# Second-layer attention of a six-layer kernel: score blocks by residue class of the query, laid between projection tiles

## Chip, cores and metric

One core of a Trainium2 chip runs one program. The metric is the device time of one execution in microseconds (us); lower is better.

## The reference, cut to what matters

Six layers, 512 tokens, width 1024, all in fp32. The change is in the second layer alone (`mixer_b`). It has 8 heads of 128 channels, and each head attends three times, with queries, keys and values of its own for each of three patterns (group g):

```python
B_PATTERNS = ((128, 1), (512, 4), (2048, 16))     # window, dilation
for g, (window, dilation) in enumerate(B_PATTERNS):
    q = apply_partial_rotary(rms_norm(qkv[:, :, 0, g], q_gain[g]), cos, sin)
    k = apply_partial_rotary(rms_norm(qkv[:, :, 1, g], k_gain[g]), cos, sin)
    o, lse = dilated_window_attention(q, k, qkv[:, :, 2, g], window // dilation, dilation)
wgt = jax.nn.softmax(jnp.stack(lses), axis=0)
o = jnp.einsum('gbsh,gbshd->bshd', wgt, jnp.stack(outs))
y = o.reshape(bsz, S, B_WIDTH).astype(h.dtype) * jax.nn.silu(z)
return y @ w_out
```

Query t of group g attends keys t - j * dilation, j = 0 to window // dilation = 128, if they exist. So group 0 ("near") sees the 129 latest tokens, group 1 every fourth token back to 512, group 2 every sixteenth. Weighting the three results by the softmax of their log-denominators equals one softmax over the union of the three groups' scores, and so the kernel does it. For groups 1 and 2 a query needs only keys of its own residue class modulo 4.

## The kernel before, in words

**Engines and signals.** Every engine has its own program, in an order written out by hand; each operation raises its engine's semaphore (`did`), and others wait for the count of an event by name (`of`). Projection weights come in 1 MB panels (1024 x 256), each a DMA on SP's queue into one of three slots of `Wr` (L326, when the panel three before is used). ACT casts a panel to `Wh` (L1225), POOL subtracts the remainder `Wl` (L344, four instructions), PE multiplies. `ahead(name)` in the ACT and POOL programs is that split, of the panel two after the one named. Products of activations and weights are three fp32r matmuls (high x high, high x low, low x high: `mm3`, L536 to L538). `tile_f` (24 matmuls of 512 columns) makes 128 features x 512 tokens in one PSUM bank; `tile_t` (48 of 256 columns; tokens are the stationary operand) makes 2 x 128 tokens x 256 features. PSUM has 8 banks: `ps` 0 to 3 and `psx` (4 to 7); `into(b)` makes PE wait until bank b is emptied.

**The second layer** runs over four pairs of heads, i = 0 to 3, each in three stages:

1. Queries and keys: 12 tiles (t = 4g + 2 * is-key + head), banks in rotation over four. ACT squares and copies each (`sq`, `tmp`, L1441, L1446), PE sums the squares over partitions with a matmul of ones (L743), ACT takes the root (L1414), DVE the reciprocal (L2008), the product with gain (L2013), the swapped half for the rotary (L2020, L2022), POOL the rest of the rotation (`rope`, L398, L401). Results are `QB` and `KB`, [channel, group, head, token].
2. Values: 6 tiles (3 groups x 2 halves of the tokens), banks in rotation over four, copied by DVE to `VB` (L2057).
3. Attention and gates. Units are (head, block j of 128 queries), j = 3 down to 0. A unit has min(2, j+1) near blocks and j+1 of each other group, 10, 8, 6 and 3 blocks of 128 x 128 (27 a head). `scores` (L760) writes them to banks 4 to 6 with one matmul a run of blocks; DVE adds the mask from `maskB` and takes the maximum (L2031), ACT the exponential with row sums (L1420), DVE the division (L2040, L2042). `flip` (L773) transposes up to four blocks into bank 7, 2 or 3, DVE and ACT in turn copy them to `tmp` (L2072, L1470), `values` (L787) multiplies with `VB` into bank 0 or 1. The next unit's scores are issued one unit ahead. The first gate tile (`z`) follows unit 0's scores, the second stands before unit 4's transposes; ACT applies silu (L1426). At the end of a head DVE multiplies with the gate (L2046), ACT casts to `Yh` (L1485), DVE subtracts to `Yl` (L1880).

Stage 1 of the next pair starts only when stage 3 is done. After the fourth pair comes the output projection `out` (8 tiles over 4 panels).

The fourth layer's attention, which the prediction also reads, contracts over 64 channels; its scores (L977) are matmuls on channels 0 to 63 and 64 to 127 of the same tiles, one of 512 and one of 256 columns in each pair. In the fifth sublayer's convolution PE transposes every second token of `wH` (L1123), an 8-byte step in its stationary operand; L1049 has such a stationary operand too, and DVE's L2395 steps by 8 bytes.

Of the kernel before, what the change touches and what calls it, by code (L numbers as in the profile page):

```python
# [104 lines left out]
B_BLOCKS = [min(2, j + 1) + 2 * (j + 1) for j in range(TT)]  # L105
B_MASK_AT = [sum(B_BLOCKS[:j]) * P for j in range(TT)]


def blocks_of(j):
    return [(0, t) for t in range(max(0, j - 1), j + 1)] + [(g, t) for g in (1, 2) for t in range(j + 1)]  # L110


B_UNITS = [(hh, j) for hh in range(2) for j in reversed(range(TT))]
B_GROUPS = [(u, q0) for u, (hh, j) in enumerate(B_UNITS) for q0 in range(0, B_BLOCKS[j], 4)]
# [69 lines left out]
def setting(nc, ctx, I):  # L184
# [38 lines left out]
    with ExitStack() as over:  # L223
# [5 lines left out]
        E.QB, E.KB, E.VB, E.maskB, E.PB, E.ropeB, E.stB = phase(  # L229
            ("QB", [P, 3, 2, S], F32), ("KB", [P, 3, 2, S], F32), ("VB", [P, 3, TT, 256], F32),  # L230
            ("maskB", [P, 27 * P], BF16), ("PB", [P, 2304], F32), ("ropeB", [32, 2, S], F32),
            ("stB", [P, TT, 4], F32))
# [23 lines left out]
    E.wsr = E.vst[:].rearrange("p a n -> p (a n)").rearrange("p (g n) -> p g n", g=8)  # L256
    E.QD, E.KD, E.VD = (E.QD0, E.QD1), (E.KD0, E.KD1), (E.VD0, E.VD1)
# [76 lines left out]
def pool_program(E, pool):  # L334
# [58 lines left out]
    def rope(i, t):  # L393
        g, qk, f = t // 4, t // 2 % 2, t % 2
        q = (E.KB if qk else E.QB)[0:32, g, f, :]
        spare = E.acc[0:32, :] if t % 2 else tmp[0:32, 3, :]
        pool.wait_ge(*V.of("B", "swap", i, t))
        pool.tensor_tensor(q, q, E.ropeB[:, 0, :], ALU.mult).then_inc(*G.did("B", "cos", i, t))  # L398
# [118 lines left out]
def pe_program(E, pe):  # L517
# [36 lines left out]
    def tile_t(p, pair, hi, lo, b, event, emptied_by, ready=None):  # L554

        into(b)
        for j, t in enumerate(pair):
            for k in range(KD):
                if ready:
                    pe.wait_ge(*ready(k))  # L560
                m = mm3(bank[b][:, j * 256:(j + 1) * 256], hi[:, k, t * P:(t + 1) * P], lo[:, k, t * P:(t + 1) * P],
                        part(E.Wh, p, k, 0, 256, KD), part(E.Wl, p, k, 0, 256, KD), k == 0, k == KD - 1)
        m.then_inc(*T.did(*event))
        emptied[b] = emptied_by
# [169 lines left out]
    def mixer_b():  # L734
        QB, KB, VB, PB = E.QB, E.KB, E.VB, E.PB
        turn = (7, 2, 3)
        norm_sums("B", "A0")

        def ssq(i, t):
            r = t % 2  # L740
            into(6 + r)
            pe.wait_ge(*A.of("B", "sq", i, t))
            pe.matmul(psx[:, 2 + r, :], ones[:], sq[:, r, :], start=True, stop=True).then_inc(*X.did("B", "ssq", i, t))  # L743
            emptied[6 + r] = A.of("B", "sqrt", i, t)

        def scores(i, u):
            hh, j = B_UNITS[u]
            for b in (4, 5, 6):
                into(b)
            if u == 0:  # L750
                pe.wait_ge(*G.of("B", "rope", i, 11))
                pe.wait_ge(*V.of("B", "v", i, 2, 1))
            runs = []
            for pos, (g, t) in enumerate(blocks_of(j)):
                if runs and runs[-1][1] == g and pos % 4:
                    runs[-1][3] += 1
                else:
                    runs.append([pos, g, t, 1])
            for pos, g, t, c in runs:
                m = pe.matmul(psf[:, pos * P:(pos + c) * P], QB[:, g, hh, j * P:(j + 1) * P], KB[:, g, hh, t * P:(t + c) * P],  # L760
                              start=True, stop=True)
            m.then_inc(*X.did("B", "s", i, u))
            for b in (4, 5, 6):
                emptied[b] = V.of("B", "sc", i, u)

        def flip(i, n):
            u, q0 = B_GROUPS[n]
            j = B_UNITS[u][1]
            po, w, b = (0 if j % 2 == 0 else 1024) + q0 * P, min(4, B_BLOCKS[j] - q0), turn[n % 3]
            into(b)  # L770
            pe.wait_ge(*V.of("B", "pn", i, u))
            for r in range(w):
                m = pe.transpose(bank[b][:, r * P:(r + 1) * P], PB[:, po + r * P:po + (r + 1) * P], ident[:])  # L773
            m.then_inc(*X.did("B", "flip", i, n))
            X.also("B", "flipped", i, u)
            emptied[b] = (A if n % 2 else V).of("B", "fe", i, n)

        def values(i, n):
            u, q0 = B_GROUPS[n]
            hh, j = B_UNITS[u]  # L780
            bl = blocks_of(j)
            if q0 == 0 and u % TT == 0:
                into(hh)
            pe.wait_ge(*(A if n % 2 else V).of("B", "fe", i, n))
            for pos in range(q0, min(q0 + 4, len(bl))):
                g, t = bl[pos]
                m = pe.matmul(bank[hh][:, j * P:(j + 1) * P], VB[:, g, t, hh * P:(hh + 1) * P],  # L787
                              tmp[:, n % 4, (pos % 4) * P:(pos % 4 + 1) * P], start=(pos == 0), stop=(pos == len(bl) - 1))
            m.then_inc(*X.did("B", "pv", i, n))
            if q0 + 4 >= len(bl) and u % TT == TT - 1:  # L790
                emptied[hh] = V.of("B", "yz", i, hh)

        for i in range(4):
            t, nb = 0, 0
            for g in range(3):
                for qk in range(2):
                    p = begin("B", "qk", i, g, qk)
                    if i + t == 0:
                        first_f("B", p, (0, 1), [("B", "qk", 0, f) for f in range(2)], [A.of("B", "cp", 0, f) for f in range(2)])
                    for f in range(2):  # L800
                        if i or t >= 2:
                            tile_f(p, f, Ah, Al, (nb + f) % 4, ("B", "qk", i, t), A.of("B", "cp", i, t))
                        if t:
                            ssq(i, t - 1)
                        t += 1
                    used(p)
                    nb += 2
            for g in range(3):
                p = begin("B", "v", i, g)
                for u in range(2):  # L810
                    tile_t(p, (2 * u, 2 * u + 1), Ah, Al, (nb + u) % 4, ("B", "v", i, g, u), V.of("B", "v", i, g, u))
                    if g + u == 0:
                        ssq(i, 11)
                used(p)
                nb += 2
            scores(i, 0)
            p = begin("B", "z", i)
            tile_f(p, 0, Ah, Al, nb % 4, ("B", "z", i, 0), A.of("B", "z", i, 0))
            for n in range(len(B_GROUPS) + 2):
                if n < len(B_GROUPS):  # L820
                    u, q0 = B_GROUPS[n]
                    if q0 == 0 and u + 1 < len(B_UNITS):
                        scores(i, u + 1)
                    if q0 == 0 and u == TT:
                        tile_f(p, 1, Ah, Al, (nb + 1) % 4, ("B", "z", i, 1), A.of("B", "z", i, 1))
                        used(p)
                    flip(i, n)
                if n >= 2:
                    values(i, n - 2)
            X.also("B", "end", i)  # L830
        T.also("h_end", "B")
        out("B", 0)
# [383 lines left out]
def act_program(E, act):  # L1216
# [180 lines left out]
    def mixer_b():  # L1397
# [3 lines left out]
        HM = 27 * P // 2  # L1401
        scale = 1.0 / float(np.sqrt(P))
        gate("A0")
        act.dma_start(PB[:, 0:HM], I["k_maskB"][:, 0:HM]).then_inc(*LDB.did(0))
        act.dma_start(qf[:, 0:HM], I["k_maskB"][:, HM:2 * HM]).then_inc(*LDB.did(1))
        act.dma_start(ropeB[:], I["k_ropeB"]).then_inc(*LDB.did(2))
        norm("B", E.Ah, "A0", summed=None)

        def sqrt(i, t):
# [4 lines left out]
            act.activation(rs[:, r, :], psx[:, 2 + r, :], ACT.Sqrt, bias=eps[:, 0:1], scale=1.0 / P).then_inc(*A.did("B", "sqrt", i, t))  # L1414

        def exp(i, u):
            hh, j = B_UNITS[u]
            po, w = 0 if j % 2 == 0 else 1024, B_BLOCKS[j] * P
            act.wait_ge(*V.of("B", "nm", i, u))
            act.activation(PB[:, po:po + w], PB[:, po:po + w], ACT.Exp, bias=stB[:, j, 1:2], scale=scale,  # L1420
                           accum_out=stB[:, j, 2:3]).then_inc(*A.did("B", "exp", i, u))

        def gates(i, f):
            act.wait_ge(*T.of("B", "z", i, f))
            act.wait_ge(*X.of("B", "ssq", i, 10 + f))
            act.activation(sq[:, f, :], ps[2 + f][:], ACT.Silu).then_inc(*A.did("B", "z", i, f))  # L1426

        for i in range(4):
            t = 0
            for g in range(3):  # L1430
                for qk in range(2):
                    for f in range(2):
                        if t:
                            sqrt(i, t - 1)
                        b = t % 4
                        act.wait_ge(*T.of("B", "qk", i, t))
                        if t >= 2:
                            act.wait_ge(*X.of("B", "ssq", i, t - 2))
                        elif i:
# [1090 lines left out]
```

## Time and profile before

| what | us |
|---|---|
| median of 3 runs (lowest, highest) | 3273.06 (3268.32, 3273.66) |
| span of the profiled execution, core 0 | 3272.5 |
| PE busy, L536 to L538, L760, L773, L787 among it | 3198.1 |
| DVE, ACT, POOL busy | 1645.0, 1102.3, 1564.8 |
| second layer, sums of squares to the output projection | 441 to 1061 |

The profile gives for the profiled execution only its span, 3272.5 us from first to last instruction, and no separate device time. A row's `L760` is the line in the kernel; `psx<-KB,QB` is output and inputs by name, the moving operand first; `x240` counts records. PE is matmuls, PEld weight loads, which overlap them. An fp32 matmul appears as two records, an fp32r one or a transpose as one. A record of a matmul is longer than the distance to the next, since they are pipelined; the pace is read from starts.

### The profile page before, as it was taken

What the parts mean: (1) busy time and instruction counts of PE and PEld (TensorE: products, weight loads), DVE (VectorE), ACT (ScalarE), POOL (GpSimd) and SP (SyncE); (2) the same over time, 40 slices, a digit from 0 to 9 for tenths busy, and PEclk for the clock granted to TensorE, in tenths of its full rate; (3) what the DMA queues carried; (4) which work ended last, traced back from release to release, by engine and by line L of the source; (5) the groups of instructions that cost most, each with busy time, mean ns of one, the idle gap of its engine ahead of it and who ended that gap; (6) DMA issues with size and microseconds to landing.
All of it is one profiled execution on the core that took longest, in us unless ns stands there. A gap on an engine that the chain in (4) does not pass through costs nothing.

```text
span 3272.5 us, 39766 instructions
## 1 busy us (share of the span) xinstructions
PE 3198.1 (98%) x16422; PEld 2643.4 (81%) x16422; DVE 1645.0 (50%) x2141; ACT 1102.3 (34%) x1449; POOL 1564.8 (48%) x1138
## 2 busy tenths in 40 slices
PE   8999999999999999999999999999999999999998
PEld 7988878787878888899887877766888867778887
DVE  6753575757474443544546666665212266542223
ACT  3221243434343332333222434444222343242222
POOL 4444475556464455454433511126545466344544
PEclk9999999999999999999999999999999999999999
DMA  5554422211221232345444211112333332223332
GB/s 165 163 165 142 142 101 65 78 65 65 65 77 53 90 103 91 103 142 179 153 147 145 70 39 39 41 37 77 104 97 97 100 124 82 80 65 94 99 96 72
DMA packets 279317, 320.07 MB, mean 98 GB/s; under 512 B 6866, under 2 KB 245089, under 8 KB 278946
## 3 DMA queue, kind: packets, MB, share of 16 engines
q1 hardware_dynamic: 240960, 247.48, 23.6%
q10 hardware_dynamic: 38178, 70.06, 6.4%
q8 instruction: 130, 2.13, 0.3%
q14 instruction: 49, 0.40, 0.0%
HBM read 311.22 MB, written 6.29 MB: 97 GB/s over the span
## 4 chain that ended last, share of the span: by engine, by line
PE 90%; DVE 4%; ACT 2%; POOL 1%; issue 1%; DMA 1%; ACTq 0%; SPq 0%; DVEq 0%
PE ps L536 25%; PE ps L538 24%; PE ps L537 24%; PE psx L977 2%; PE psx L743 1%; PE ps L1009 1%; POOL Wl L344 1%; PE ps L787 1%; PE psx L721 1%; PE psx L536 1%; PE psx L537 1%; PE psx L538 1%; PE psx L636 1%; PE psx L760 1%; PE psx L688 1%
## 5 line engine op out<-in xcount | busy, mean ns | idle before, releaser
L344 POOL TENSOR_TENSOR Wl<-Wr,Wh 128x512 fp32r<-128x512 f32 x928 | 1281.5, 1413 | 1506.5 <-ACT Wh L1225 1502.4
L536 PE MATMUL ps<-Ah,Wh 128*128 128x512 f32 x1920 | 771.5, 402 | 0.7 <-POOL Wl L344 0.7
L538 PE MATMUL ps<-Ah,Wl 128*128 128x512 f32 x1920 | 748.4, 390 | 0.0
L537 PE MATMUL ps<-Al,Wh 128*128 128x512 f32 x1920 | 747.9, 390 | 0.0
L1225 ACT ACTIVATE Wh<-Wr 128x2048 fp32r<-128x2048 f32 x232 | 443.0, 1910 | 368.6 <-DMA Wr<-in_w_mlp_in_dram 109.8
L536 PEld LDWEIGHTS ps<-Ah,Wh 128*128 128x128 f32 x1920 | 360.7, 188 | 85.0 <-issue 11.1
L537 PEld LDWEIGHTS ps<-Al,Wh 128*128 128x128 f32 x1920 | 360.7, 188 | 83.3 <-issue 10.3
L536 PE MATMUL ps<-Yh,Wh 128*128 128x512 f32 x1088 | 425.1, 391 | 0.1
L537 PE MATMUL ps<-Yl,Wh 128*128 128x512 f32 x1088 | 423.8, 390 | 0.0
L538 PE MATMUL ps<-Yh,Wl 128*128 128x512 f32 x1088 | 423.7, 389 | 0.0
L538 PEld LDWEIGHTS ps<-Ah,Wl 128*128 128x128 f32 x1920 | 360.4, 188 | 76.6
L536 PE MATMUL ps<-Wh,Ah 128*128 128x256 f32 x896 | 257.6, 288 | 3.3 <-DVE vA L1936 3.3
L538 PE MATMUL ps<-Wh,Al 128*128 128x256 f32 x896 | 253.5, 283 | 0.0
L537 PE MATMUL ps<-Wl,Ah 128*128 128x256 f32 x896 | 253.4, 283 | 0.0
L536 PEld LDWEIGHTS ps<-Yh,Wh 128*128 128x128 f32 x1088 | 204.7, 188 | 42.8 <-issue 0.4
L538 PEld LDWEIGHTS ps<-Yh,Wl 128*128 128x128 f32 x1088 | 204.5, 188 | 42.8
L537 PEld LDWEIGHTS ps<-Yl,Wh 128*128 128x128 f32 x1088 | 204.6, 188 | 41.9
L1924 DVE SCALAR_TENSOR_TENSOR macc<-modw,sc,macc 128x512 f32<-128x512 f32 x168 | 166.3, 990 | 115.3 <-DMA modw<-in_w_mod_dram 108.8
L2008 DVE RECIPROCAL rs<-rs 128x512 f32<-128x512 f32 x48 | 160.6, 3346 | 44.3 <-ACT rs L1414 44.2
L536 PEld LDWEIGHTS ps<-Wh,Ah 128*128 128x128 f32 x896 | 171.8, 192 | 5.6 <-issue 5.6
L537 PEld LDWEIGHTS ps<-Wl,Ah 128*128 128x128 f32 x896 | 171.9, 192 | 1.9 <-issue 1.9
L538 PEld LDWEIGHTS ps<-Wh,Al 128*128 128x128 f32 x896 | 171.9, 192 | 0.0
(405 smaller groups left out, 4157.7 us busy)
## 6 DMA issues: line engine op xcount, KB each, us to landing
Wr<-in_a_w_in_dram SPq DMA_DIRECT2D x48, 1024.0 KB, 6.7
modw<-in_w_mod_dram ACTq DMA_DIRECT2D x96, 512.0 KB, 5.5
Wr<-in_b_w_in_dram SPq DMA_DIRECT2D x40, 1024.0 KB, 5.0
Wr<-in_w_mlp_in_dram SPq DMA_DIRECT2D x32, 1024.0 KB, 5.5
Wr<-in_w_mlp_out_dram SPq DMA_DIRECT2D x32, 1024.0 KB, 5.1
Wr<-in_a_w_out_dram SPq DMA_DIRECT2D x16, 1024.0 KB, 5.2
Wr<-in_c_w_in_dram SPq DMA_DIRECT2D x16, 1024.0 KB, 5.6
Wr<-in_attn_w_qkv_dram SPq DMA_DIRECT2D x12, 1024.0 KB, 5.2
```

The lines of the kernel that those rows point to most:

```text
L344: last = pool.tensor_tensor(E.Wl[:, s, part], E.Wr[:, s, part], E.Wh[:, s, part].bitcast(F32), ALU.subtract)
L536: pe.matmul(o, ah, bh, start=first, stop=False)
L537: pe.matmul(o, ah, bl, start=False, stop=False)
L538: return pe.matmul(o, al, bh, start=False, stop=last)
L636: pe.matmul(psx[:, 2, 0:cols], ones[:], sq[:, k % 2, 0:cols], start=(k == 0), stop=(k == KD - 1)).then_inc(*X.did(*event))
L688: m = pe.matmul(psx[:, 1, c:c + 1], t[:, r * P:(r + 1) * P], ones[:, 0:1], start=True, stop=True)
L721: m = pe.matmul(psx[:, 2 * f, t * P:(t + 1) * P], E.vst[:, f, t * P:(t + 1) * P], E.wsT[:, q, :], start=True, stop=True)
L743: pe.matmul(psx[:, 2 + r, :], ones[:], sq[:, r, :], start=True, stop=True).then_inc(*X.did("B", "ssq", i, t))
L977: m = pe.matmul(psf[:, c:c + k1 - k0], q[64 * r:64 * r + 64, h, j * P:(j + 1) * P], k[64 * r:64 * r + 64, h, k0:k1], start=True, stop=True)
L1225: act.activation(E.Wh[:, s, :], E.Wr[:, s, :], ACT.Copy).then_inc(*HI.did(p))
L1924: dve.scalar_tensor_tensor(t, w, E.sc2[:, k, who:who + 1], t, ALU.mult, ALU.add).then_inc(*V.did("mac", L, nb, who, k))
L2008: dve.reciprocal(rs[:, r, :], rs[:, r, :]).then_inc(*V.did())
```

## The change

Units become (head, residue class r of the query modulo 4), 8 a pair of heads. A unit's 128 queries are the tokens 4n + r. Groups 1 and 2 need one block each, the keys of class r; the near group needs, for each quarter q of the unit's queries (32 of them, tokens 128q to 128q + 127), the token blocks q - 1 and q (0 and 1 for q = 0, masked). That is four blocks a unit, 16 a head, and one PSUM bank. The near scores are four matmuls of 32 stationary columns each, one for each quarter, into partitions 32q to 32q + 31.

To this end `QB` (all groups) and `KB` (groups 1 and 2) are stored class by class, by a stepped read in DVE's product; near keys stay in token order, and the rotary tables are ordered by class. The values of groups 1 and 2 are computed by `tile_t` with the tokens of a class (every fourth) as stationary operand. The mask is 4 x 512 columns a partition in place of 3456.

The order changes: units stand between the last four value tiles and the two gate tiles; the last two units' transposes and values of a pair, and its second head's output, stand between the first three query tiles of the next pair (`tail`), for the fourth pair inside the output projection, whose first three tiles are cut by k into 0 to 5, 6 and 7. Query and key tiles rotate over banks 0 to 2, value tiles over 0 and 1, gates take 0 and 1, the heads' outputs 2 and 3, scores and sums of squares 4 and 5, transposes 6 and 7. ACT alone empties the transposes; it copies the gate tiles out and applies silu to both at the end of the stage. DVE multiplies output and gate with stepped access. The POOL program has the same steps; only the near keys' rotation is stepped.

The diff, cut to its core:

```diff
+def by_class(ap):
+    return ap.rearrange("a (r n) -> a r n", r=4)
+def by_token(ap):
+    return ap.rearrange("a (n r) -> a r n", r=4)
+def near(ap, q):
+    return ap.rearrange("a (r q n) -> a q r n", r=4, q=4)[:, q]
# POOL, rope
-        pool.tensor_tensor(q, q, E.ropeB[:, 0, :], ALU.mult)
+        turn = by_token if qk and g == 0 else by_class
+        pool.tensor_tensor(turn(q), turn(q), by_class(E.ropeB[:, 0, :]), ALU.mult)
# PE
+        def qk(i, t):
...
+                tile_f(p, f, Ah, Al, t % 3, ("B", "qk", i, t), A.of("B", "cp", i, t))
...
+            if t:
+                ssq(i, t - 1)
+        def value(i, n):
+            g, u = n // 2, n % 2
...
+            if g:
+                tile_t(p, (2 * u, 2 * u + 1), Ah, Al, u, event, V.of(*event), lambda a, r: by_token(a)[:, r])
+            else:
+                tile_t(p, (2 * u, 2 * u + 1), Ah, Al, u, event, V.of(*event))
+        def scores(i, u):
+            hh, r = u // 4, u % 4
+            b, c0 = 4 + u % 2, u % 4 * P
+            into(b)
+            if r == 0:
+                pe.wait_ge(*G.of("B", "rope", i, 10 + hh))
+            for q in range(4):
+                t = max(q - 1, 0)
+                pe.matmul(bank[b][32 * q:32 * q + 32, 0:256], QB[:, 0, hh, c0 + 32 * q:c0 + 32 * q + 32], KB[:, 0, hh, t * P:(t + 2) * P], start=True, stop=True)
+            for g in (1, 2):
+                m = pe.matmul(bank[b][:, (g + 1) * P:(g + 2) * P], QB[:, g, hh, c0:c0 + P], KB[:, g, hh, c0:c0 + P], start=True, stop=True)
+        def far(i, u):
...
+            for g in (1, 2):
+                pe.matmul(bank[2 + hh][:, r * P:(r + 1) * P], VB[:, g, r, hh * P:(hh + 1) * P], E.PT[hh][:, r, (g + 1) * P:(g + 2) * P],
+                          start=(r == 0 and g == 1), stop=False)
+        def close(i, hh):
+            for q in range(4):
+                for c in range(2 if q else 1):
+                    t = max(q - 1, 0) + c
+                    m = pe.matmul(near(bank[2 + hh], q), VB[:, 0, t, hh * P:(hh + 1) * P], E.PT[hh][:, :, c * P + 32 * q:c * P + 32 * q + 32],
+                                  start=False, stop=(q == 3 and c == 1))
+        def tail(i, n):
+            if n < 2:
+                flip(i, 6 + n)
+                far(i, 5 + n)
+            if n == 2:
+                far(i, 7)
+                close(i, 1)
         for i in range(4):
+            for t in range(12):
+                qk(i, t)
+                if i:
+                    tail(i - 1, t)
+            value(i, 0)
+            ssq(i, 11)
+            value(i, 1)
+            for n in range(B_UNITS):
+                if n < 4:
+                    value(i, n + 2)
+                elif n % 2 == 0:
+                    gate(i, n // 2 - 2)
+                scores(i, n)
+                if 1 <= n < 7:
+                    flip(i, n - 1)
+                if n == 4:
+                    far(i, 0)
+                    far(i, 1)
+                elif n == 5:
+                    far(i, 2)
+                    far(i, 3)
+                    close(i, 0)
+                elif n == 6:
+                    far(i, 4)
+        for c in range(3):
+            part_out(c, 0, 6)
+            tail(3, c)
+        for c in range(3):
+            part_out(c, 6, 7)
+        for c in range(3):
+            part_out(c, 7, 8)
# DVE
+            near_keys = qk and g == 0
+            put = by_token if near_keys else by_class
-            dve.scalar_tensor_tensor(dst, tmp[:, t % 3, :], pk(E, "b_k_gain" if qk else "b_q_gain", g), rs[:, r, :],
+            dve.scalar_tensor_tensor(put(dst), by_token(tmp[:, t % 3, :]), pk(E, "b_k_gain" if qk else "b_q_gain", g), by_token(rs[:, r, :]),
         for i in range(4):
             for t in range(11):
                 rest(i, t)
+                if i and t == 1:
+                    y(i - 1, 1)
+            rest(i, 11)
+            for n in range(2):
+                value(i, n)
+            for n in range(B_UNITS):
+                if n < 4:
+                    value(i, n + 2)
+                scores(i, n)
+                weights(i, n)
+            y(i, 0)
```

## Rows read from the trace of the kernel before

**Rows 1.** The page: busy time by engine, and the granted clock in 40 slices.

```profile
PE 3198.1 (98%) x16422; PEld 2643.4 (81%) x16422; DVE 1645.0 (50%) x2141; ACT 1102.3 (34%) x1449; POOL 1564.8 (48%) x1138
PEclk9999999999999999999999999999999999999999
```

**Rows 2.** Stretches: length, busy time (records) of PE, PEld, DVE, ACT, POOL, clock, DMA.

```profile
441.00:517.20 76.20, 76.20 (x356) 60.61 (x357) 69.00 (x57) 31.96 (x42) 65.96 (x46) 1.00 0.26 84
...
541.79:587.79 46.00, 42.12 (x271) 36.94 (x271) 21.87 (x50) 21.50 (x32) 6.88 (x6) 1.00 0.14 46
...
1014.60:1060.80 46.20, 42.06 (x271) 36.93 (x271) 21.97 (x51) 21.50 (x32) 6.58 (x5) 1.00 0.15 46
```

**Rows 3.** PE timeline around the first attention stage: start, duration, engine, line.

```profile
540.63 0.28 PE L538 MATMUL ps<-Wh,Al 128*128 128x256 f32 x1
...
543.83 0.58 PE L536 MATMUL ps<-Ah,Wh 128*128 128x512 f32 x1
...
549.49 1.89 PE L760 MATMUL psx<-KB,QB 128*128 128x256 f32 x8
...
587.74 0.48 PE L536 MATMUL ps<-Ah,Wh 128*128 128x512 f32 x1
```

**Rows 4.** Chain of waits: start, duration, what (x: records).

```profile
556.77 0.86 DVE PB L2031
557.86 1.04 ACT PB L1420 x2
559.12 0.63 DVE PB L2042
...
562.52 2.17 PE psx L760 x10
...
575.75 0.44 PE psx L773 x4
...
583.44 0.89 PE ps L787 x8
...
598.88 0.86 PE psx L743 x2
```

**Rows 5.** PE timeline at the end of the first value tile.

```profile
510.87 0.28 PE L537 MATMUL ps<-Wl,Ah 128*128 128x256 f32 x1
510.99 0.28 PE L538 MATMUL ps<-Wh,Al 128*128 128x256 f32 x1
511.11 1.02 PE L743 MATMUL psx<-sq,ones 128*128 128x512 f32 x2
```

**Rows 6.** DVE timeline: end of the query and key stage, and one product later.

```profile
512.89 3.35 DVE L2008 RECIPROCAL rs<-rs 128x512 f32<-128x512 f32 x1 [0.40 <-ACT rs L1414]
...
519.75 1.27 DVE L2057 COPY VB<-ps 128x512 f32<-128x512 f32 x2
...
610.24 0.75 DVE L2013 SCALAR_TENSOR_TENSOR QB<-tmp,PK,rs 128x512 f32<-128x512 f32 x1
```

**Rows 7.** PE and PEld timelines, fourth layer's first scores (split by 64 rows).

```profile
1874.25 2.33 PE L977 MATMUL psx<-KD,QD 64*128 64x512 f32 x8
1876.50 0.50 PE L536 MATMUL ps<-Ah,Wh 128*128 128x512 f32 x1
...
1875.44 0.30 PEld L977 LDWEIGHTS psx<-KD,QD 64*128 64x128 f32 x4 [0.90 <-PE psx L977]
```

**Rows 8.** Single lines: duration in ns least/median/most, first and last start.

```profile
L1123 PEld LDWEIGHTS psx<-ident,wH x32: 195/209/209, 2712.8 to 2779.4; 128*128 128x128 f32 x32
...
L773 PEld LDWEIGHTS psx<-ident,PB x84: 137/140/144, 550.9 to 1058.7; 128*128 128x128 f32 x84
...
L1049 PEld LDWEIGHTS psx<-woF,hdX x16: 189/193/193, 2135.1 to 2189.3; 64*128 64x128 f32 x16
...
L787 PEld LDWEIGHTS ps<-tmp,VB x432: 186/192/192, 553.7 to 1060.7; 128*128 128x128 f32 x144
...
L2395 DVE TENSOR_TENSOR Yl<-psx,Yh x4: 679/680/680, 2824.8 to 2830.7; 128x512 fp32r<-128x512 f32 x4
```

More of the change, by code:

```diff
@@ L102 @@
     pass
[L105 to L114, printed above, removed]
+B_UNITS = 8
+def by_class(ap):
[4 more added lines that the diff above has]
+    return ap.rearrange("a (r q n) -> a q r n", r=4, q=4)[:, q]
 D_HEADS = 8
@@ L740, in ssq @@
             r = t % 2
-            into(6 + r)
+            into(4 + r)
             pe.wait_ge(*A.of("B", "sq", i, t))
-            pe.matmul(psx[:, 2 + r, :], ones[:], sq[:, r, :], start=True, stop=True).then_inc(*X.did("B", "ssq", i, t))
-            emptied[6 + r] = A.of("B", "sqrt", i, t)
-        def scores(i, u):
[L747 to L761, printed above, removed]
-            m.then_inc(*X.did("B", "s", i, u))
-            for b in (4, 5, 6):
-                emptied[b] = V.of("B", "sc", i, u)
@@ L770, in flip @@
+        def flip(i, u):
+            b = 6 + u % 2
             into(b)
             pe.wait_ge(*V.of("B", "pn", i, u))
[L772 to L791, printed above, removed]
@@ L793, in mixer_b @@
-        for i in range(4):
[L794 to L830, printed above, removed]
@@ new lines, in part_out @@
+        def part_out(c, k0, k1):
+            p = E.at["B", "o", 0, c // 2]
+            if c % 2 == 0 and k0 == 0:
+                begin("B", "o", 0, c // 2)
+            for k in range(k0, k1):
+                if k == 0:
+                    into(c)
+                pe.wait_ge(*V.of("B", "y", 0, k))
+                m = mm3(bank[c], part(E.Wh, p, k, c % 2 * P, c % 2 * P + P, KD), part(E.Wl, p, k, c % 2 * P, c % 2 * P + P, KD), Yh[:, k, :], Yl[:, k, :],
+                        k == 0, k == KD - 1)
+            if k1 == KD:
+                m.then_inc(*T.did("B", "o", 0, c))
+                emptied[c] = V.of("B", "o", 0, c)
@@ new lines, in gate_in, with gates @@
+        def gate_in(i, f):
+            act.wait_ge(*T.of("B", "z", i, f))
+            if f == 0:
+                act.wait_ge(*X.of("B", "ssq", i, 10))
+            elif i:
+                act.wait_ge(*V.of("B", "y", 0, 2 * i - 1))
+            act.activation(E.gateB[f], ps[f][:], ACT.Copy).then_inc(*A.did("B", "zc", i, f))
+        def gates(i):
+            act.wait_ge(*A.of("B", "zc", i, 1))
+            for f in range(2):
+                act.activation(E.gateB[f], E.gateB[f], ACT.Silu).then_inc(*A.did("B", "z", i, f))
@@ new lines, in tail @@
+        def tail(i, n):
+            if n < 2:
+                turned(i, 6 + n)
+            if n == 2:
+                y(i, 1)
+        for i in range(4):
+            for t in range(12):
+                if t:
+                    sqrt(i, t - 1)
+                qk(i, t)
+                if i:
+                    tail(i - 1, t)
+            ahead("B", "v", i, 0)
+            sqrt(i, 11)
+            for n in range(B_UNITS):
+                if n in (4, 6):
+                    gate_in(i, n // 2 - 2)
+                if 1 <= n < 7:
+                    turned(i, n - 1)
+                exp(i, n)
+                if n in (1, 3):
+                    ahead("B", "v", i, (n + 1) // 2)
+                if n == 5:
+                    ahead("B", "z", i)
+            gates(i)
+            y(i, 0)
@@ L1479, in mixer_b @@
+        for n in range(3):
+            tail(3, n)
         out("B", 0, True, x, "B")
```

246 lines of the change are left out of this document (111 added, 135 removed).

## The prediction

> **What bounds the kernel now.** I read the page first: PE is busy for 3198.1 us of 3272.5, at a granted clock of nine tenths or more nearly everywhere [rows 1]. So only what PE does, or waits for, has a price; other engines matter where they make PE wait. Then the stretches of the second layer. In its query and key stage PE is busy for all of 76.20 us, DVE for 69.00, POOL for 65.96; in the attention stage that follows PE is busy for 42.1 of 46.0, DVE and ACT for less than half, and the clock is 1.00 [rows 2]. The four attention stages are alike (46.0, 45.9, 46.0 and 46.2 us; first and last in [rows 2]).
>
> The PE timeline gives one stage's true length: the last value matmul starts at 540.63, and they follow each other at 0.12, so the stage runs from 540.75 to the next query tile at 587.74: 47.0 us [rows 3, 5]. Of that the two gate tiles are 2 x 5.66 (543.83 to 549.49) and stay. 35.7 us remain for attention proper. The chain gives PE's paces, an fp32 matmul being two records: five of 256 columns in 2.17 (0.43 each), four transposes in 0.44 (0.11), four value matmuls of 128 in 0.89 (0.22); a 512-column one takes 0.86 [rows 4, 5]. A stage has 54 blocks (27 a head, two heads): scores 54 x 0.217 = 11.7, transposes 54 x 0.11 = 5.9, values 54 x 0.22 = 12.0, together 29.6. The other 6.1 us are latencies and waits: for the value copy, then for the DVE, ACT, DVE softmax chain.
>
> **The change, part by part, per stage.**
> *Transposes*: 8 units of 4 blocks: 32 x 0.11 = 3.5 (before 5.9). *Values*: far 16 x 0.22 = 3.6; near 7 a head, 14 x 0.22 = 3.1 (before 12.0 together). *Far scores*: 16 x 0.217 = 3.5.
> *Near scores*: per unit four matmuls of 32 weight columns and 256 moving ones, into four partition quarters. No column split is in the trace. One after another they cost 4 x 0.43 = 1.73. The nearest row is the fourth layer's split by 64 contraction rows: pairs of 512 and 256 columns. In sequence a pair would stream for 0.86 + 0.43 = 1.29; the two pairs run from 1874.25 to 1876.50, the second from 1875.44, so 1.06 us, entering and leaving included [rows 7]. The longer matmul's 0.86 plus 0.2: the halves ran together, and 0.2 is the price of a change of split. I carry that over: 0.43 + 0.2 = 0.63 a unit, 5.1 a stage; the other end is 1.73 + 0.2, 15.4 a stage.
> [...]
> *Waits removed*: the 6.1 us, as each unit's softmax now runs under a value or gate tile of 5.7 us or more. The chain is 3.1 us for 768 columns (scores from 556.77, weights done 559.75) [rows 4], so it is covered there.
> *Waits added*, two:
> (a) Value tiles now alternate over banks 0 and 1 in place of four. The third waits for DVE's copy of the first, queued behind the last two query/key chains. In the trace value tile one ends at 511.11, the sum of squares takes 0.86, tile two 48 x 0.12 = 5.76: PE is free at 517.7. DVE does both copies as a pair from 519.75, the first done at 520.4 [rows 5, 6]. Stall 2.7. Queued behind that waiting matmul is everything on PE.
> (b) Unit 4's transposes stand after only unit 3's transposes, four far value matmuls and unit 5's scores: 0.44 + 0.89 + 1.07 = 2.4 us for a chain of about 2.8 at 512 columns, plus 0.25 as ACT first empties unit 3. Stall 0.65. Unit 6's have a gate tile.
> *The seam*: units 6 and 7 and the head's second output go between the next stage's first three tiles. On PE it is work already counted. DVE gets a product and a subtraction of 0.7 each with ACT's cast between, 2.2 us, in a stage where PE then has 76.2 + 3.7 us; DVE's 69.0 busy (plus gaps) still fits. In the end stage the output tiles are cut in three so that the last output comes in time; its latency of 2.2 us meets 2.1 of matmuls: nothing.
> *DMA, POOL and ACT queues*: panels keep their order and number; a panel's slot is freed as before or, with the output panel, some 6 us later, under 16 us of matmuls. The mask load shrinks, before the first tile. ACT's table loads fall; ACT has room.
> *Strides*. DVE now reads two operands and POOL one group of keys at a 16-byte step, and 16 of the 24 value tiles load weights so: tokens four apart. Nothing in the trace steps by 16 bytes. Steps of 8 bytes are there. DVE at 8 bytes: 0.680 us, like its plain operations. PE, plain fp32 weights at 8 bytes: 193 ns against 186 to 192 for plain ones. But transposes' weights: 209 against 140 [rows 8]. So one row says steps are free at this loading speed and one says that loads which are fast when packed are not when stepped. Lower end 0 (a step cannot make a load faster than packed). Upper end: the 209 is 0.07 us above packed, where the same values lie over twice the bytes. At 16 bytes they lie over twice that again: 0.07 more if each doubling costs the same, 0.14 if each byte spanned does; in the middle 0.11. Nothing hides it: value matmuls are 0.12 apart although 256 columns should stream in half of a gate matmul's 0.236 (5.66 / 24), so loads set their pace already. 0.11 x 48 = 5.3 us a tile, 21 a stage. I take 0, by the plain-load row, as these too are plain loads; it is the weakest term here.
>
> Sum of a stage: 3.5 + 3.6 + 3.1 + 3.5 + 5.1 + 2.7 + 0.65 = 22.1 in place of 35.7, so 13.6 less; four stages 54. The profiled execution spans 3272.5, the median is 3273.1, the same to 0.02%. Forecast **3218**.
>
> **Rivals.**
> *A, stepped weight loads at half speed (slower).* Place: value tiles three to six of each stage. The 54 are gained, 4 x 21 = 84 paid, and since DVE's stepped reads would slow as well, some 2 us a stage are added to wait (a): 3273 - 54 + 84 + 8 = **3311**. It decides from 54 / 768 loads = 0.070 us a load, 0.19 us apart. For it: the 140 to 209 row. Against: the 193 row, where 8 bytes cost nothing.
> [...] I give A nearly two chances in five.
> *B, near scores in sequence.* 32 x 1.3 = 42 back: **3260**, still faster. Against it: rows 7. With A it would be 3353.
> *C, a partial stepping cost*, about half of A's: 3273 - 54 + 42 = **3261**; from 0.062 to 0.079 us a load it is no measurable difference.
> *D, DVE bound.* If the stepped product takes 0.75 more than its 0.75 [rows 6] while weights cost nothing, a DVE step of 5.75 busy (69.0 / 12) and some 0.3 of gaps becomes 6.8 against PE's 6.35 (76.2 / 12). Over 12 steps DVE falls 5.4 behind, less 1.5 at a seam: about 4 us a stage into wait (a): **3234**. DVE's 0.68 at 8 bytes speaks against it.
>
> **How the numbers follow.** Forecast or D: 0.45; B: 0.08; C: 0.10, of which 0.04 within 0.2%; A: 0.33; A with B or worse: 0.04. 0.2% (6.5 us) is about what a measurement of this kernel can tell from no change. Faster 0.58, same 0.04, slower 0.38. The likeliest case by itself spans 3208 (waits (a) and (b) half as long) to 3234. The range must take in A, as both signs hold much of the chance: 3208 to 3316; A with B, and A at 0.14 a load (3334), are left out.
>
> **What would show it.** Right: the stepped value tiles still 0.12 us apart, near scores starting four at a time with a unit's scores near 1.1 us, PE idle about 2.7 us before the third value tile for the value copy and under 1 us before unit 4's transposes, stages (value end to next query tile, value and gate tiles taken out) of 22 us. Wrong: stepped weight loads above 0.19 us apart (then A, and slower), score groups of 2.3 us (B), DVE with no idle time through the query and key stage (D), or a wait on POOL's rotation before unit 0.

## The result, and the profile after

**3320.7 us** (median of 4 runs, 3319.7 to 3321.4) against 3271.9 of the kernel before (4 runs, 3268.3 to 3273.7): ratio 1.0147, 95% interval 1.0135 to 1.0159. The change costs 48.8 us; the forecast was a gain of 54. The profiled execution spans 3319.4 us. The page, to set beside [rows 1]:

```profile
PE 3241.0 (98%) x16286; PEld 2677.9 (81%) x16286; DVE 1628.6 (49%) x2108; ACT 1083.6 (33%) x1445; POOL 1583.9 (48%) x1138
PEclk9999999999999999999999999999999999999999
```

PE does 136 matmul records fewer and is busy 43 us longer, so the work that remains has become slower. The second layer's attention stages are where to look. Stretches of the changed kernel (columns as in [rows 2]): the query and key stage with the first two value tiles, the idle time before the third, and what follows it:

```profile
441.30:517.00 75.70, 74.88 (x350) 59.20 (x350) 71.05 (x56) 31.93 (x42) 67.23 (x44) 1.00 0.25 82
517.00:522.70 5.70, 1.05 (x9) 0.85 (x9) 5.44 (x7) 0.00 (x0) 5.62 (x4) 0.94 0.53 184
522.70:529.40 6.70, 6.67 (x28) 6.70 (x29) 0.48 (x1) 0.00 (x0) 6.62 (x6) 0.54 0.00 0
529.40:533.00 3.60, 3.60 (x17) 3.60 (x16) 0.00 (x0) 0.00 (x0) 0.00 (x0) 1.00 0.00 0
```

PE stands still for most of the second stretch; then it works for 6.7 us at a mean clock of 0.54: 0.50 in every us up to 528.70, and 0.92 in the 0.7 after it. DVE, idle for 7.2 us of the 76.20 of the query and key stage before [rows 2], is idle for 4.65 of the 75.70 now. The PE timeline of the same kernel, to set beside [rows 3, 5]:

```profile
522.73 0.57 PE L546 MATMUL ps<-Wh,Ah 128*128 128x256 f32 x1 [4.68 <-DVE VB L2089]
523.09 0.44 PE L547 MATMUL ps<-Wl,Ah 128*128 128x256 f32 x1
523.33 0.44 PE L548 MATMUL ps<-Wh,Al 128*128 128x256 f32 x1
...
534.16 0.64 PE L793 MATMUL psx<-KB,QB 128*32 128x256 f32 x8
534.73 0.71 PE L795 MATMUL psx<-KB,QB 128*128 128x128 f32 x4
535.20 0.48 PE L546 MATMUL ps<-Wh,Ah 128*128 128x256 f32 x1
...
565.35 0.40 PE L546 MATMUL ps<-Wh,Ah 128*128 128x256 f32 x1
565.58 0.40 PE L547 MATMUL ps<-Wl,Ah 128*128 128x256 f32 x1
565.81 0.40 PE L548 MATMUL ps<-Wh,Al 128*128 128x256 f32 x1
...
583.67 0.63 PE L804 MATMUL psx<-ident,PB 128*128 128x128 f32 x4 [0.28 <-DVE PB L2107]
...
607.19 1.02 PE L750 MATMUL psx<-sq,ones 128*128 128x512 f32 x2
```

Four things are to be read here. The value tiles of the far keys, whose loads step, run at one matmul every **0.233 us** (565.35, 565.58, 565.81) where they ran at 0.12 [rows 5]. The wait for the value copy is **4.68 us**, not 2.7 (3.63, 3.63 and 3.67 in the other three stages). The four 32-column near scores take **0.57 us** together (534.16 to 534.73; 0.63 forecast). The wait before unit 4's transposes is **0.28** (0.65 forecast). From one stage's first sum of squares to the next it is now 167.2 to 167.8 us (157.7 before), so some 10 us of each stage are lost.

The layer can also be measured by itself, from its first sum of squares to the first matmul behind its output projection that waits for its operand. Before:

```profile
440.98 1.10 PE L743 MATMUL psx<-sq,ones 128*128 128x512 f32 x2 [0.55 <-ACT sq L1441]
...
1114.57 0.73 PE L577 MATMUL ps<-Al,Wh 128*128 128x512 f32 x2 [0.72 <-POOL Al L355]
```

and after:

```profile
439.95 1.10 PE L750 MATMUL psx<-sq,ones 128*128 128x512 f32 x2 [0.55 <-ACT sq L1475]
...
1163.33 0.74 PE L585 MATMUL ps<-Al,Wh 128*128 128x512 f32 x2 [0.73 <-POOL Al L364]
```

That is 673.6 us before and 723.4 after: the 49.8 us lost lie inside the layer. This length is the better measure for the experiments, since what lies outside it differs by up to 8 us from one kernel's profiled execution to another's (2591.8 to 2600.1 us), mostly behind the layer, where no experiment edits anything.

The loads by form, from the groups of the second layer's stretch, 420 to 1230 us. Stepped loads and the plain ones of the near value tiles lie together in these groups:

```profile
L546 PE MATMUL ps<-Wh,Ah 128*128 128x256 f32 x384 | 143.2, 373 | 15.6 <-DVE VB L2089 15.6
L546 PEld LDWEIGHTS ps<-Wh,Ah 128*128 128x128 f32 x384 | 108.7, 283 | 18.6 <-issue 18.0 <-POOL Wl L353 0.7
```

All four waits (a) are in the first row: 15.6 us. A load's mean is 283 ns, where a packed one took 192 [rows 8]. Of these 384 loads 256 step; they take 0.33 us each, as the timeline of PE's weight loads in the changed kernel has it ((128 x 192 + 256 x 330) / 384 = 284):

```profile
530.20 0.33 PEld L548 LDWEIGHTS ps<-Wh,Al 128*128 128x128 f32 x1
530.43 0.33 PEld L546 LDWEIGHTS ps<-Wh,Ah 128*128 128x128 f32 x1
```

### The profile page after: what moved, and what is told of

It reads as the page before. It is cut to its first block, busy times and chain, and to the rows that moved or that the text cites. A ratio compares the mean times of both kernels' runs of the same rounds, so it can differ in the third digit from the quotient of the medians.

```text
span 3319.4 us, 39338 instructions
## 1 busy us (share of the span) xinstructions
PE 3241.0 (98%) x16286; PEld 2677.9 (81%) x16286; DVE 1628.6 (49%) x2108; ACT 1083.6 (33%) x1445; POOL 1583.9 (48%) x1138
## 4 chain that ended last, share of the span: by engine, by line
PE 82%; DVE 11%; issue 2%; ACT 2%; POOL 2%; DMA 1%; ACTq 0%; DVEq 0%; SPq 0%
PE ps L546 22%; PE ps L548 22%; PE ps L547 22%; DVE rs L2066 5%; PE psx L1032 2%; POOL Wl L353 1%; PE ps L1064 1%; DVE KB L2073 1%; DVE QB L2073 1%; PE psx L729 1%; PE psx L546 1%; PE psx L547 1%; PE psx L548 1%; PE psx L644 1%; PE psx L696 1%
## 5 line engine op out<-in xcount | busy, mean ns | idle before, releaser
L546 PE MATMUL ps<-Wh,Ah 128*128 128x256 f32 x896 | 289.0, 323 | 19.0 <-DVE VB L2089 15.6
L547 PE MATMUL ps<-Wl,Ah 128*128 128x256 f32 x896 | 283.6, 316 | 0.0
L548 PE MATMUL ps<-Wh,Al 128*128 128x256 f32 x896 | 283.5, 316 | 0.0
L546 PEld LDWEIGHTS ps<-Wh,Ah 128*128 128x128 f32 x896 | 207.0, 231 | 22.3 <-issue 21.7
L547 PEld LDWEIGHTS ps<-Wl,Ah 128*128 128x128 f32 x896 | 207.3, 231 | 1.7 <-issue 1.7
L548 PEld LDWEIGHTS ps<-Wh,Al 128*128 128x128 f32 x896 | 207.3, 231 | 0.0
```

The costliest lines, as they stand in the source:

```text
L546: pe.matmul(o, ah, bh, start=first, stop=False)
L547: pe.matmul(o, ah, bl, start=False, stop=False)
L548: return pe.matmul(o, al, bh, start=False, stop=last)
```

## The experiments

The times in the order of the text, and the length of the layer in each profiled execution:

| kernel | time, us | layer, us |
|---|---|---|
| before | 3271.9 (3273.4 to 3274.1 beside the experiments) | 673.6 |
| the change | 3320.7 | 723.4 |
| 1 packed loads | 3244.1 | 643.0 |
| 2 before, stepped | 3359.1 | 762.5 |
| 3 step of 8 / 12 bytes | 3241.5 / 3278.7 | 643.3 / 680.4 |
| 4 three banks | 3306.6 | 708.2 |
| 5 plain product | 3310.9 | 715.2 |
| 6 near scores in sequence | 3349.6 | 753.1 |
| 7 early cast | 3313.7 | 717.5 |
| 8 values by DMA | 3243.0 | 642.8 |
| 9 and three banks | 3214.4 | 619.4 |
| 10 and early cast | 3208.0 | 613.1 |
| 11 and ACT's sorting | 3205.5 | 611.3 |

**1. The same tiles with packed loads.** The far value tiles read tokens side by side:

```diff
-                tile_t(p, ..., event, V.of(*event), lambda a, r: by_token(a)[:, r])
+                tile_t(p, ..., event, V.of(*event))
```

> The changed kernel, but all value tiles load tokens that lie side by side (the far groups' values are then those of other tokens, so this part of the result differs). Theory, stepped weight loads: the 768 stepped loads are 0.233 us apart in the changed kernel's timeline and 0.120 without the step, so the time falls by 768 x 0.113 = 87 us, from 3321 to about 3234, and below the kernel before. Rival, the new order and DVE's stepped reads cost the time: the loads hide behind something else and it stays above 3300.

Measured: **3244.1 us** (3241.2 to 3247.2), ratio to the kernel before 0.9911 [0.9894, 0.9927]. The sign turns with this one edit: 77 us come back, 80.4 of them in the layer. By the paces it would be 87; where the other 7 of the layer are, experiments 8 and 9 show.

**2. The reverse: the kernel before with stepped loads.** Its value tiles after the first two take tokens four apart, the rest stays:

```diff
+                    every = (lambda a, r: a.rearrange("a (n r) -> a r n", r=4)[:, r]) if g else ...
-                    tile_t(p, ..., V.of("B", "v", i, g, u))
+                    tile_t(p, ..., V.of("B", "v", i, g, u), None, every)
```

> The kernel before, with nothing changed but the step: the 16 far value tiles load every fourth token (the result differs in that part). Theory: 768 loads x 0.113 us = 87 us more, about 3359 for 3272. Rival, the step costs only in the new order: under 10 us more.

Measured: **3359.1** (three runs, 3358.8 to 3360.9; a fourth took 9169.4, for which nothing on record gives a reason, and is left out), ratio 1.0261 [1.0243, 1.0278]: 85.5 us for 768 loads, 0.111 us each. The layer is 88.9 us longer. Its PE timeline:

```profile
555.31 0.40 PE L536 MATMUL ps<-Wh,Ah 128*128 128x256 f32 x1
555.54 0.40 PE L537 MATMUL ps<-Wl,Ah 128*128 128x256 f32 x1
```

The pace is the changed kernel's 0.233, with nothing else of the change there. So the price belongs to the step.

**3. Which step costs.** The changed kernel with far tiles that read every second token (8 bytes), then every third (12 bytes):

```diff
-                ..., lambda a, r: by_token(a)[:, r])
+                ..., lambda a, r: a[:, 256 * (r // 2):256 * (r // 2) + 256].rearrange("a (n r) -> a r n", r=2)[:, r % 2])
```

> The changed kernel, but far value tiles load tokens two apart (an 8-byte step; other tokens, so the result differs). Theory by the row of 193 ns against 190: an 8-byte step costs a plain load nothing, the loads are 0.120 apart and the time is that of the packed ones, about 3244. Rival, the cost grows evenly with the step: 0.158 apart (a third of the way from 4 to 16 bytes), about 3270.

```diff
+                ..., lambda a, r: a[:, 32 * r:32 * r + 384].rearrange("a (n r) -> a r n", r=3)[:, 0])
```

> The same with tokens three apart (12 bytes). [...] Rival, a threshold at 16 bytes: 0.120 apart, about 3244; or a threshold above 8 bytes: 0.233 apart, about 3321.

Measured: 8 bytes **3241.5** (ratio 0.9903 [0.9889, 0.9918]), 12 bytes **3278.7** (1.0018 [1.0008, 1.0027]). PE timeline with 8 bytes:

```profile
530.00 0.28 PE L546 MATMUL ps<-Wh,Ah 128*128 128x256 f32 x1
530.12 0.28 PE L547 MATMUL ps<-Wl,Ah 128*128 128x256 f32 x1
```

and with 12:

```profile
530.13 0.34 PE L546 MATMUL ps<-Wh,Ah 128*128 128x256 f32 x1
530.31 0.34 PE L547 MATMUL ps<-Wl,Ah 128*128 128x256 f32 x1
```

Steps of 4 and 8 bytes give 0.120 us a matmul, 12 give 0.173, 16 give 0.233. So the pace at 12 bytes is neither of the two that the thresholds of its rival give (0.120, 0.233). A load reads 128 values of 4 bytes from each partition; at 8, 12 and 16 bytes of step these lie over 1024, 1536 and 2048 bytes. The last two paces divide out to 0.113 and 0.114 ns a byte. By that, 1024 bytes would be 0.116 us, just under the packed pace of 0.120, and this would be why the plain load at 8 bytes in [rows 8] looked free. It is an estimate from two points; what in a load takes this time, no run shows.

**4. Wait (a): a third bank.** The value tiles go round three accumulator banks:

```diff
-                tile_t(p, (2 * u, 2 * u + 1), Ah, Al, u, event, ...)
+                tile_t(p, (2 * u, 2 * u + 1), Ah, Al, n % 3, event, ...)
-            dve.tensor_copy(VB[...], ps[u][:]...)
+            dve.tensor_copy(VB[...], ps[n % 3][:]...)
```

> The changed kernel with value tiles in rotation over banks 0, 1, 2 in place of 0 and 1. Theory: the wait before the third value tile (idle 4.68, 3.63, 3.63, 3.67 us) goes, as the fourth tile has another 11 us; the time falls by 14 to 17 us, to about 3305. Rival: DVE is late for whatever comes next (unit 0's softmax, the copies), so the wait reappears at the fourth tile or at unit 0's transposes and less than 5 us are won.

Measured: **3306.6**, ratio 1.0098 [1.0083, 1.0114]: 14.1 us back (15.2 in the layer), against 15.6 of idle time. The idle time is nearly all, and no clock comes back with it here. Its PE timeline has, where 4.68 stood,

```profile
517.98 0.51 PE L546 MATMUL ps<-Wh,Ah 128*128 128x256 f32 x1 [0.23 <-POOL Wl L353]
```

**5. Why wait (a) is longer than forecast: DVE's product plain.**

```diff
-            dve.scalar_tensor_tensor(put(dst), by_token(tmp[...]), ..., by_token(rs[...]), ...)
+            dve.scalar_tensor_tensor(dst, tmp[...], ..., rs[...], ...)
```

> The changed kernel, but DVE's product reads and writes in order, with no 16-byte step (queries and far keys are then not sorted by class, so the result differs). Theory: the product falls from 1.12 us at best back to 0.75, DVE is on time at the end of the query and key stage, the wait before the third value tile falls from 3.6 to 4.7 us to about 2.7, and the time by 4 to 8 us, to about 3314. Rival, DVE is what the change made the bound: the time falls by 25 us or more.

Measured: **3310.9**, ratio 1.0113 [1.0098, 1.0129]: 10 us back, 8.2 of them in the layer. The PE timeline's first wait becomes

```profile
518.37 0.48 PE L546 MATMUL ps<-Wh,Ah 128*128 128x256 f32 x1 [2.51 <-DVE VB L2089]
```

and the others 2.00 each. In the changed kernel the product's durations are

```profile
L2073 DVE SCALAR_TENSOR_TENSOR QB<-tmp,PK,rs x24: 1122/1312/1984, 446.2 to 1009.7; 128x512 f32<-128x512 f32 x24
```

so at its best it takes 1.12 us where the plain one takes 0.75 [rows 6]. DVE still had time to spare in the stage, but the value copy stands behind the last products in its queue, and their lateness is the copy's. The four waits now make 8.5 us in place of 15.6, so 7.1 of the 8.2; an idle time of 0.82 at 479.92, on a panel's split, is gone as well. The other 2 us of the 10 lie outside the layer. With plain products wait (a) is 2.0 to 2.5: the forecast's 2.7 was about right for the kernel that it had in mind, and the stepped operands made it 3.9 on average.

**6. Near scores one after another.** Full width in place of 32 columns, four times in sequence:

```diff
-                pe.matmul(bank[b][32 * q:32 * q + 32, 0:256], QB[:, 0, hh, c0 + 32 * q:c0 + 32 * q + 32], KB[...], ...)
+                pe.matmul(bank[b][:, 0:256], QB[:, 0, hh, c0:c0 + P], KB[...], ...)
```

> The changed kernel, but the four near matmuls of a unit use all 128 columns of weights each and write over one another, so that they run in sequence (the near scores are then partly wrong). Theory: the four column strips run side by side (0.57 us a unit in the changed kernel's timeline); in sequence they take 4 x 0.43 = 1.73, so 32 x 1.16 = 37 us more, about 3358. Rival, the strips gained nothing: no difference.

Measured: **3349.6**, ratio 1.0231 [1.0214, 1.0248], 28.9 above the changed kernel (29.7 in the layer). Its PE timeline:

```profile
533.03 1.89 PE L793 MATMUL psx<-KB,QB 128*128 128x256 f32 x8
534.75 0.61 PE L795 MATMUL psx<-KB,QB 128*128 128x128 f32 x4
```

1.72 us in place of 0.57: the quarters do run side by side, three times as fast as in sequence. 32 x 1.15 would be 37. By the starts, the far scores behind a full-width group take 0.37 (534.75 to 535.12), behind the quarters 0.47; over a whole stage they take 3.4 us and 4.4. The wait before unit 4's transposes (0.28) is gone, as the longer scores of unit 5 cover it, and the matmul ahead of a unit is 0.24 from it in place of 0.33 (532.79 to 533.03; 533.83 to 534.16). That is 1.0, 0.3 and 0.4 a stage, 6.8 of the 7.3 us missing in the layer.

**7. The output end.** The forecast priced the late panel there at nothing. The PE timeline of the changed kernel:

```profile
1129.77 0.79 PE L546 MATMUL ps<-Yh,Wh 128*128 128x512 f32 x1 [4.37 <-POOL Wl L353]
```

and its ACT and POOL timelines ahead of that:

```profile
1119.35 0.63 ACT L1339 ACTIVATE sq<-x 128x512 f32<-128x512 f32 x1 [2.50 <-DVE x L1908]
1121.34 0.63 ACT L1339 ACTIVATE sq<-x 128x512 f32<-128x512 f32 x1 [1.36 <-DVE x L1908]
1121.88 1.90 ACT L1280 ACTIVATE Wh<-Wr 128x2048 fp32r<-128x2048 f32 x1
...
1123.86 10.80 POOL L353 TENSOR_TENSOR Wl<-Wr,Wh 128x512 fp32r<-128x512 f32 x8 [27.92 <-ACT Wh L1280]
```

The cast of the third output panel stands in ACT's queue behind the squares of the first output tiles, which wait for DVE (2.50, 1.36). POOL, idle for 27.92 us, can split only after it. The edit issues that cast ahead of ACT's cast of the last head's output:

```diff
-            ahead(L, "o", half, n)
+            if L != "B" or n:
+                ahead(L, "o", half, n)
...
+            if n == 2:
+                ahead("B", "o", 0, 0)
```

> The changed kernel, but ACT casts the third output panel before the last head's output and not behind the first output tile's square. Theory: PE's idle time of 4.37 us before that panel goes, 3321 - 4.5 = about 3316. Rival: the panel was late by DMA or POOL: nothing changes.

Measured: **3313.7** (3311.6 to 3315.8), ratio 1.0123 [1.0108, 1.0138]: 7.1 us back, 5.9 of them in the layer, for an idle time of 4.37, which is gone. The other 1.5 of the layer fit what follows it: after the idle time the mean clock in the changed kernel was 0.50 from 1129.8 to 1133.0.

**8. The change kept, the step moved to a transfer.** PE reads tokens side by side; DVE copies a far value tile to a buffer, and DMAs from ACT's queue move its partitions to their classes, 8 a stage, 32 partitions each:

```diff
+            dst = E.PTB[:, n - 2, :] if g else VB[:, g, 2 * u:2 * u + 2, :]...
+            dve.tensor_copy(dst, ps[u][:])...
...
+                act.dma_start(E.VB[32 * t:32 * t + 32, g, :, :], E.PTB[:, n - 2, 256 * j:256 * j + 256])...
```

> The changed kernel, complete, but the far values are computed with tokens side by side and sorted into classes by DMA (8 a stage, rows of 1 KB, from the buffer of the last transposes to VB, issued by ACT). Theory: the stepped loads go as with packed weights and the sorting hides under the gate tile: 3321 - 77 = about 3244. Rival: the DMAs land too late for the first far values at unit 4, or slow the weight panels: PE idle before unit 4's values, 3255 or more.

Measured: **3243.0** (3240.3 to 3246.2), ratio 0.9912 [0.9896, 0.9929]. The transfers land 3.4 us after their issue, without an idle time of PE to show for it: this is the time of experiment 1, and its layer is as long (642.8, 643.0). So it has the same 7 us too many. Its stretch behind wait (a), and the PE timeline in it:

```profile
521.40:527.20 5.80, 5.80 (x30) 5.80 (x31) 0.42 (x1) 0.00 (x0) 5.72 (x6) 0.56 0.00 0
```

```profile
522.15 0.41 PE L546 MATMUL ps<-Wh,Ah 128*128 128x256 f32 x1
522.36 0.41 PE L547 MATMUL ps<-Wl,Ah 128*128 128x256 f32 x1
...
526.84 0.28 PE L548 MATMUL ps<-Wh,Al 128*128 128x256 f32 x1
526.96 0.28 PE L546 MATMUL ps<-Wh,Ah 128*128 128x256 f32 x1
```

After 4.72 us of idle time packed loads are 0.21 apart for some 5 us at a clock of 0.56, then 0.12 again. In the 5 us behind the other three waits the mean clock is 0.66, 0.66 and 0.71. In the changed kernel the same clock cost next to nothing, since stepped loads are 0.236 apart at 0.54 and 0.233 at 1.00.

**9. Is it the clock?** The kernel of 8 with three banks, nothing more (the two edits of 4). Either only the idle time comes back, or the half-speed stretch behind it as well:

> The kernel with values sorted by DMA (3243), with value tiles over three banks and nothing else. Theory: each wait before the third value tile costs its idle time (4.72, 3.67, 3.72, 3.69) and after it a stretch at half the clock, in which the packed value tile that follows runs at half its pace; without the waits both go, about 26 us, to 3217. Rival, only the idle time counts: 16 us, 3227.

Measured: **3214.4** (5 runs, 3214.1 to 3216.1), ratio 0.9819 [0.9806, 0.9833]: 28.6 us below experiment 8, against 15.8 of idle time. Its stretches from the third value tile on:

```profile
516.00:522.00 6.00, 5.79 (x49) 5.58 (x48) 5.74 (x6) 0.00 (x0) 5.92 (x5) 1.00 0.53 172
522.00:528.00 6.00, 6.00 (x55) 5.46 (x54) 3.40 (x8) 0.82 (x2) 5.93 (x5) 1.00 0.07 23
```

Without the wait the clock stays at 1.00 and PE does 55 matmuls in 6 us, not 30 in 5.8. In the layer 23.4 us come back (642.8 to 619.4), so each wait of 3.6 to 4.7 us cost 1.9 us more behind it ((23.4 - 15.8) / 4); in a whole stage the value tiles' matmuls take 35.9 us where they took 37.6. The other 5 of the 28.6 lie outside the layer, where this edit changes nothing: so the 26 expected were nearly met in the sum, but the share of the slow clock in them was 10, and 7.6 were measured. The fall comes behind each of the four waits of experiment 8, with the mean clocks given there (0.56, 0.66, 0.66 and 0.71).

**10. All three.** The kernel of 9 with the early cast of 7 (their edits together, no other line):

> The same with value tiles over three banks and the third output panel cast early. If the three gains add: 3244 - 14 - 7 = about 3223. Rival: with tiles at 5.8 us in place of 11.2 DVE is late for the fourth value tile, so part of the 14 us stays: 3230 or more.

Measured: **3208.0** (3206.7 to 3209.4), ratio 0.9802 [0.9787, 0.9817], 15 us below the 3223 expected. Half of that is the slow clock behind the waits (7.6 by experiment 9), which the sum of the three gains left out; most of the rest lies outside the layer. Besides 0.83 us at 479.75, PE has only these idle times in the four stages, the first in the first stage alone, the second in each:

```profile
518.11 0.39 PE L546 MATMUL ps<-Wh,Ah 128*128 128x256 f32 x1 [0.20 <-POOL Wl L353]
557.03 0.63 PE L804 MATMUL psx<-ident,PB 128*128 128x128 f32 x4 [0.28 <-DVE PB L2120]
```

**11. And DVE's steps to ACT.** ACT's square and copy sort by class as they leave the accumulator, so that DVE's product is plain:

```diff
-            act.activation(tmp[:, t % 3, :], ps[t % 3][:], ACT.Copy)...
+            act.activation(dst(tmp[:, t % 3, :]), src(ps[t % 3][:]), ACT.Copy)...
-            dve.scalar_tensor_tensor(put(dst), by_token(tmp[...]), ..., by_token(rs[...]), ...)
+            dve.scalar_tensor_tensor(dst, tmp[...], ..., rs[...], ...)
```

> The same, and ACT's square and copy do the sorting by class (stepped reads of PSUM) in place of DVE's product. Theory: DVE's product is 0.75 us at best again, its lateness at the end of the stage goes, 3 to 8 us less than with DVE's stepped reads. Rival: ACT slows as much (0.6 us operations near 1 us) and delays the sums of squares: same or slower.

Measured: **3205.5** (3205.3 to 3205.8), ratio 0.9794 [0.978, 0.9809], the fastest of all: 68 us below the kernel before in the same series (3273.4) and 115 below the change as it stood. Against experiment 10 that is 2.6 us, a little less than the 3 to 8 expected. The layer is 1.7 shorter, all of it in the first stage (140.8 to 139.1); the others were at 141.9 already. With three banks PE had no wait left there on DVE's product but, in the first stage, two on panels' splits (0.8 and 0.2), which are gone. The product is back at its plain duration:

```profile
L2087 DVE SCALAR_TENSOR_TENSOR QB<-tmp,PK,rs x24: 752/850/1585, 446.4 to 928.2; 128x512 f32<-128x512 f32 x24
```

and ACT's sorted reads cost it nothing (groups by form, 430 to 1080 us, of the same kernel; 601 and 592 ns in the changed one):

```profile
L1483 ACT ACTIVATE tmp<-ps 128x512 f32<-128x512 f32 x48 | 28.7, 598 | 0.0
L1478 ACT ACTIVATE sq<-ps 128x512 f32<-128x512 f32 x48 | 28.4, 592 | 6.6 <-PE ps L585 4.2 <-DVE Yl L1955 2.5
```

## Why the prediction was wrong

**The step that failed is "Strides": "I take 0, by the plain-load row, as these too are plain loads".** The measured price is 0.113 us a load by the starts, 87 us in all, next to the 0.11 that the same paragraph put in the middle of its bounds (0 to 0.14). The 193 ns row of [rows 8] was read as "a step is free for plain loads". It only said that an 8-byte step is; the same row also fits a cost of 0.11 ns for each byte that the values lie over (the estimate of experiment 3), which stays hidden until it passes the packed pace of 0.120 us. The row that spoke the other way, 140 to 209 ns for transposes, was there, and rival A, which rests on it, was given less than two chances in five. The same mistake was made for DVE: its 0.68 us at 8 bytes stood for 16 bytes too, where experiment 5 shows 1.12. To decide between two rows that disagree I should have asked which one has slack in it: the load that takes 186 to 192 ns when packed showed no cost at 8 bytes (193), the one that takes 140 did (209).

Rival A was the case that came true, at 3311 and with its place right. It was 10 us short. In the layer it forecast 38 us more (84 + 8 - 54), and 49.8 were measured, 12 short:

- *Loads*: 84 forecast. By the starts the matmuls of the value tiles take 58.2 us in a whole stage, 35.5 before, so 22.7 a stage and 91 in all: 7 more. 87 of it is the pace; the rest is mostly the step from a tile to a unit between two tiles and back, 0.33 in place of 0.233 each way (533.83 to 534.16).
- *Wait (a)*: 2.7 plus A's 2 a stage, so 8 us for the four beyond the forecast; measured 3.9 on average, 1.2 beyond, so 5, which is 3 less.
- *Output end*: "nothing". It cost 4.4 of idle time and some 1.5 of slow clock (5.9 by experiment 7). The step that failed there is "under 16 us of matmuls": it compared the panel's slot with PE's work and did not ask where the cast stands in ACT's own queue, behind squares that wait for the last output.
- *Attention itself*. In a whole stage the units' matmuls take 18.8 us by the starts and the wait of (b) 0.28, where the terms of the forecast without wait (a) make 19.4: 1 less in all. In it the near scores were put too high (4.6 measured, 5.1) and the far scores too low (4.4 measured, 3.5). The stage before had 30.5 of work and 4.7 of waits, 35.2 and not 35.7: 2 more in all.

Together 7 - 3 + 6 - 1 + 2 = 11 us of the 12. What lies outside the layer was 3 us shorter in the changed kernel's profiled execution (2596.0) than in the other's (2598.9).

Two of the prediction's numbers do not come out of its own terms, and neither matters here: the chain from 556.77 to 559.75 is 2.98 us, not 3.1, and with waits (a) and (b) half as long the forecast is 3211, not 3208.

What was right: near scores (0.63 forecast, 0.57), unit 4's wait (0.65, 0.28), the seam (no idle time of PE there), DVE not the bound in the query and key stage, and nearly the size of the gain. D's mechanism was there in part, though: the stepped product took 0.37 more at its best, not 0.75, and made wait (a) 1.8 us a stage longer (experiment 5), where D had 4. Experiment 10 has the change without its three faults. By the forecast's terms without wait (a) it would be 3272 - 54 - 11 = 3207, and 3208.0 was measured; but the layer is 60.5 us shorter where those terms have 65, and the rest of the fall lies outside it, so the agreement to 1 us is partly luck. Even with free loads the forecast of 3218 would not have been met: experiment 8 has them and took 3243.0. Its layer is 30.8 us shorter than before, 23 less than the forecast's 54: wait (a)'s extra length (5), the slow clock behind the waits (8 by experiment 9), the output end (6), and 4 more, of which the 2 above (35.2 in place of 35.7 a stage) are a part and 2 stay open.

The range missed by 5 us because its high end was A's own figure plus 5. A case with a third of the chance needed an uncertainty of its own on that side, for the unknown waits above all.

## What to carry to other kernels

Before a layout puts a step into an operand, ask for each engine that reads it how much slack its present pace has over that step: for fp32 weight loads 8 bytes were free (0.120 us), and 16 bytes took a matmul with 256 moving columns from 0.120 to 0.233 us; DVE's product went from 0.75 to 1.12. Put a reordering where it is free (here ACT's copy out of the accumulator, 598 ns against 601, or a 3.4 us transfer beside other work), not into the bound engine's reads. A wait of PE of about 4 us cost half as much again as its length (23.4 us for 15.8) where packed loads came behind it. And ask of a buffer's refill where it stands in its engine's own queue, not only when its slot comes free: here the cast behind two squares cost PE 4.37 us.

## What the runs showed that was not expected

- Weight loads of value tiles: 0.120 us a matmul at 4 and 8 bytes of step, 0.173 at 12 and 0.233 at 16.
- A stepped load's pace hardly moves with the clock: 0.236 us apart at 0.54 and 0.233 at 1.00, where packed ones go from 0.12 to 0.21.
- DVE's product with two operands in the buffer at a 16-byte step takes 1.12 us at best in place of 0.75; ACT, reading the accumulator at that step and writing in order, stays at 0.60.
- Four matmuls of 32 weight columns and 256 moving ones take 0.57 us, the four in sequence 1.72; each small load takes 108 ns in the changed kernel:

```profile
L793 PEld LDWEIGHTS psx<-KB,QB x256: 106/108/110, 534.2 to 1097.7; 128*32 128x32 f32 x128
```
